# A streaming encoder layer on one core: the opening stages in another order (pool inputs first, in 2 KB rows; forget columns last; input tiles normed and transposed one by one)

## The reference, cut to what matters

```
h = rmsnorm(x, g_mix_pre)                      # x is (384, 2048)
p = h @ w_in                                   # w_in is (2048, 8208)
q, k, v = p[:, 0:1024], p[:, 1024:2048], p[:, 2048:3072]
logf = log_sigmoid(p[:, 3072:3088] + b_f)      # forget columns, one per head
u = p[:, 3088:4112]                            # pool inputs, 4 groups of 256 columns
ga, gb = p[:, 4112:6160], p[:, 6160:8208]
a_out  = softmax(q k^T / 8 + c[t] - c[s]) v    # c = cumulative sum of logf (cache_logf before it)
pooled = windowed means of u (2, 4, 8, 16 rows, with state_pool before it) - u
m = sigmoid(ga) * (a_out @ w_attn_up) + sigmoid(gb) * (pooled @ w_pool) * pool_scale
x = x + rmsnorm(m @ w_out);  y = x + rmsnorm(relu(rmsnorm(x) @ w_ff1)^2 @ w_ff2)
```

## Time and profile before

| | us |
|---|---|
| three runs | 1989.45, 1991.40, 1992.78 |
| median of the runs | 1991.4 |
| profiled execution, its own time | 1990.38 |
| profiled execution, its span | 1988.8 |
| PE busy in the span | 1925.6 |

### The profile page before, as it was taken

How to read it: one execution, slowest core, us unless ns; L and a number is a source line. 1 busy time by engine, 2 the same in 40 slices (tenths; PEclk the granted TensorE clock), 3 DMA queues, 4 the chain that set the end, 5 groups by cost and what they waited for, 6 DMA issues and landing times.

```text
span 1988.8 us, 26585 instructions
## 1 busy us (share of the span) xinstructions
PE 1925.6 (97%) x10576; PEld 1782.7 (90%) x10576; DVE 843.0 (42%) x1064; ACT 661.9 (33%) x896; POOL 188.8 (9%) x242
## 2 busy tenths in 40 slices
PE   3999999999999999997999999999999999999997
PEld 3998999989999998886989989899899898998996
DVE  4644444444333324336444444444444444444446
ACT  4333443433323323335323323223233232232332
POOL 0623323320010102001000000000000000000000
PEclk8999999999999999998999999999999999999999
DMA  6537878855434435342344344343443444434432
GB/s 164 141 94 203 174 193 172 181 149 127 127 127 127 128 127 205 129 128 90 126 129 127 128 127 127 128 127 127 128 127 128 127 127 128 127 127 128 127 127 86
DMA packets 216315, 269.40 MB, mean 135 GB/s; under 512 B 15313, under 2 KB 150705, under 8 KB 215184
## 3 DMA queue, kind: packets, MB, share of 16 engines
q1 hardware_dynamic: 200912, 235.98, 41.6%
q0 software_dynamic: 15296, 31.90, 5.3%
HBM read 260.69 MB, written 7.08 MB: 135 GB/s over the span
## 4 chain that ended last, share of the span: by engine, by line
PE 93%; DMA 3%; DVE 1%; issue 1%; ACT 1%; POOL 1%; SPq 0%; DVEq 0%; ACTq 0%; POOLq 0%
PE ps L459 18%; PE ps L461 18%; PE ps L460 18%; PE ps L479 11%; PE ps L480 11%; PE ps L481 11%; DMA w_raw<-in_w_in_dram 1%; DMA bias_s<-ncs_dram 1%; PE ps L614 1%; DMA out_dram<-u_nat 1%; PE ps L680 0%; PE ps L631 0%; PE ps L835 0%; PE ps L685 0%; DVE w_lo L1261 0%
## 5 line engine op out<-in xcount | busy, mean ns | idle before, releaser
L1261 DVE TENSOR_TENSOR w_lo<-w_raw,w_hi 128x1024 fp32r<-128x1024 f32 x437 | 544.6, 1247 | 864.5 <-ACT w_hi L905 864.3
L905 ACT CAST w_hi<-w_raw 128x1024 fp32r<-128x1024 f32 x437 | 458.5, 1050 | 894.1 <-PE ps L461 453.3
L459 PE MATMUL ps<-ht_hi,w_hi 128*128 128x384 f32 x2064 | 697.6, 338 | 4.8 <-DVE w_lo L1261 3.0
L461 PE MATMUL ps<-ht_hi,w_lo 128*128 128x384 f32 x2064 | 691.1, 335 | 0.0
L460 PE MATMUL ps<-ht_lo,w_hi 128*128 128x384 f32 x2064 | 690.9, 335 | 0.0
L459 PEld LDWEIGHTS ps<-ht_hi,w_hi 128*128 128x128 f32 x2064 | 388.7, 188 | 7.8 <-issue 7.2
L460 PEld LDWEIGHTS ps<-ht_lo,w_hi 128*128 128x128 f32 x2064 | 388.7, 188 | 0.4
L461 PEld LDWEIGHTS ps<-ht_hi,w_lo 128*128 128x128 f32 x2064 | 388.3, 188 | 0.0
L479 PE MATMUL ps<-w_hi,z_hi 128*128 128x512 f32 x762 | 298.8, 392 | 1.8 <-DVE w_lo L1261 1.8
L480 PE MATMUL ps<-w_lo,z_hi 128*128 128x512 f32 x762 | 300.2, 394 | 0.0
L481 PE MATMUL ps<-w_hi,z_lo 128*128 128x512 f32 x762 | 295.7, 388 | 0.0
(11 more groups left out here) (241 smaller groups left out, 1133.2 us busy)
## 6 DMA issues: line engine op xcount, KB each, us to landing
w_raw<-in_w_ff_dram SPq DMA_DIRECT2D x256, 512.0 KB, 3.7
w_raw<-in_w_in_dram SPq DMA_DIRECT2D x130, 512.0 KB, 6.5
w_raw<-in_w_out_dram SPq DMA_DIRECT2D x32, 512.0 KB, 3.7
kc<-in_cache_k_dram POOLq DMA_DIRECT2D x8, 1024.0 KB, 12.3
vc<-in_cache_v_dram POOLq DMA_DIRECT2D x8, 1024.0 KB, 11.7
w_raw<-in_w_attn_up_dram SPq DMA_DIRECT2D x16, 512.0 KB, 3.6
bias_s<-ncs_dram POOLq DMA_DIRECT2D x64, 48.0 KB, 6.8
out_dram<-z_gain SPq DMA_DIRECT2D x6, 512.0 KB, 2.7
```

Of the source, the lines that this page charges most:

```text
L459: pe.matmul(out, wh[:, k, cols], x_hi[:, kk, :], start=(kk == 0), stop=False)
L461: last = pe.matmul(out, wl[:, k, cols], x_hi[:, kk, :], start=False, stop=(kk == k_last))
L905: nc.scalar.copy(w_hi[:, u % RING, :], w_raw[:, u % RAWS, :]).then_inc(hi_ready, 1)
L1261: nc.vector.tensor_tensor(w_lo[:, u % RING, :], w_raw[:, u % RAWS, :], f32(w_hi[:, u % RING, :]), ALU.subtract).then_inc(lo_ready, 1)
```

## The change

The numbers of the units are permuted: `U_U = 0`, `U_F = U_U + 16`, `U_POOL = U_F + 2`. The pool inputs are taken as two halves of eight units with 2 KB rows. The forget chain comes after the pool inputs, spread over the pool stage and the first head pair. What the kernel computes is the same.

```diff
 # SP
-            for t in range(TT):
-                sp.dma_start(x_sb[:, t, :], ...)
             sp.dma_start(gain_nat[:, 0, :], ...)
+            for t in range(2):
+                sp.dma_start(x_sb[:, t, :], xp_v[:, t, :]).then_inc(x_landed[t], 16)
+            sp.dma_start(x_sb[:, 2, 0:D // 2], xs_v[:, 0:D // 2]).then_inc(x_landed[2], 16)
+            sp.dma_start(x_sb[:, 2, D // 2:D], xs_v[:, D // 2:D]).then_inc(x_half_landed, 16)
+            def pool_inputs(g):
+                for q in range(8):
+                    load(U_U + 8 * g + q, 0, win(2 * q, 2, OFF_U + 512 * (1 - g), 512), 2, 512)
+            pool_inputs(0)
             (gain rows 1 and 2)
+            pool_inputs(1)
             for n in range(2):
                 load(U_F + n, 0, win(8 * n, 8, OFF_F, P), 8, P)
-            for s, g in enumerate(ORDER):
-                for n in range(4):
-                    load(U_U + 4 * s + n, 0, win(4 * n, 4, OFF_U + 256 * g, 256), 4, 256)
 # PE
             pe.wait_ge(pool_const, 1)
+            for n in range(10):
+                pe.transpose(ps[:, 0, 0:P], ident[:, :], ident[:, :])
+            (gain row 0 turned) 
+            for n in range(20):
+                pe.transpose(ps[:, 0, 0:P], ident[:, :], ident[:, :])
+            pe.wait_ge(gain_ready, 1)
+            for t in range(TT):
+                pe.wait_ge(xn_ready, t + 1)
+                for k in range(8):
+                    turn_x(t, k)
+                if t < TT - 1:
+                    for n in range(16 - 8 * t):
+                        pe.transpose(ps[:, 7, 3 * P:4 * P], ident[:, :], ident[:, :])
+            for q in range(8):
+                pe.wait_ge(ht_lo_ready, max(4, 2 * q + 2))
+                across(U_U + q, 0, 4, 4, 2 * q, 2, ht_hi, ht_lo, KD - 1)
+                (q < 4: k-tiles 8 + 2q and 9 + 2q turned; q == 6: state, cached logf, gains turned)
+            pe.wait_ge(hist_saved, 2)
+            pe.wait_ge(aux_saved, 2)
+            for q in range(8):
+                across(U_U + 8 + q, 0, 0, 4, 2 * q, 2, ht_hi, ht_lo, KD - 1)
+            for n in range(2):
+                across(U_F + n, 0, 7, 1, 8 * n, 8, ht_hi, ht_lo, KD - 1)
 ...
             pe.wait_ge(brb_act, 2 * GROUPS)
+            head_pair(U_HP, 0, 0, 0, False)
             pe.wait_ge(brb_dve, 2 * GROUPS)
             pe.wait_ge(unat_saved, 4)
-            head_pair(U_HP, 0, 0, 0, False)
+            pe.wait_ge(f_dve, 12)
+            (logf turned, then_inc(fnat_psum, 1)); pe.wait_ge(fnat_saved, 1)
 # ACT
+            act.wait_ge(ones_ready, 1)
+            nc.scalar.activation(root_warm[:, :], ones[:, 0:TT], ACT.Sqrt)
+            (squares: tile 2 only its first half)
             slot(-2, 0)
+            for k in range(4):
+                turned_hi(k)
             slot(-1, 0)
+            (turned_hi 4 to 7; then slot(U_U + q) and two turned_hi for q in 0 to 3)
 ...
+            slot(U_F, 0); slot(U_F + 1, 0)
+            pool_hi(2, ORDER[2])
+            act.wait_ge(f_dve, 3)
+            (f_exp; aux_saved; then U_POOL, with f_log at s == 2)
             head_pair(U_HP, 0, 0, 0, False)
             act.wait_ge(pool_stored, 144)
             act.wait_ge(nc_stored, 144)
+            act.wait_ge(logf_stored, 32)
             head_pair(U_HP + 6, 0, 1, 1, True)
 # DVE
+            (tile 2: tensor_tensor_reduce squares its second half; the tile is scaled in two halves)
+            turned_lo 0, 1; slot(-2); turned_lo 2, 3; slot(-1); turned_lo 4 to 7; then per unit two
 ...
+            slot(U_F, 0); slot(U_F + 1, 0)
+            pool_lo(2, ORDER[2])
+            f steps 1 to 3
+            slot(U_POOL); outs(0); pool_lo(3); slot(U_POOL + 1); f step 4; outs(1); f steps 5 to 7
+            slot(U_POOL + 2); outs(2); un_p and u_nat copies; slot(U_POOL + 3); outs(3)
+            f steps 8 to 12; ncp scan
+            slot(U_HP, 0)
+            slot(U_HP + 1, 0)
+            new_forgets()          # waits logf_new_in 128 and aux_saved; scan, seven copies
+            slot(U_HP + 2, 0)
+            slot(U_HP + 3, 0)
+            keys(0, 0)
+            slot(U_HP + 4, 0)
+            slot(U_HP + 5, 0)
+            (fnat_psum; logf_nat copied out, fnat_saved)
             head_pair(U_HP + 6, 0, 1, 1, True)
 # POOL
-            (b_f, state and cached logf loads first)
+            nc.gpsimd.memset(ones[:, :], 1.0).then_inc(ones_ready, 1)
             (identity, iotas)
+            pool.wait_ge(x_landed[TT - 1], 16)
+            (state, cached logf, b_f loads)
+            (all four windows; nine stores of u)
             pool.wait_ge(unit_used, U_HP)
+            load_keys(0)
+            load_values(0)
             pool.wait_ge(pool_stored, 144)
             (memsets of qp and qs, q_zero)
+            pool.wait_ge(f_dve, 12)
+            for b in range(BD):
+                pool.dma_start(logf_all[...], logf_t[...]).then_inc(logf_new_in, 16)
+            pool.wait_ge(ncp_ready, 1)
+            pool.dma_start(ncp_dram, ncp[:, :]).then_inc(nc_stored, 16)
+            pool.wait_ge(ncs_ready, 2)
+            for b in range(BD):
+                pool.dma_start(ncs_dram[:, b, :, :], ncs[...]).then_inc(nc_stored, 16)
             pool.wait_ge(nc_stored, 144)
             pool.wait_ge(dve_const, 11)
-            load_keys(0)
             load_bias(0)
-            load_values(0)
+            pool.wait_ge(fnat_saved, 1)
+            pool.dma_start(lfp_v, logf_nat[:, 0:2, :]).then_inc(logf_stored, 16)
+            pool.dma_start(lfs_v, logf_nat[:, 2, :]).then_inc(logf_stored, 16)
```

More of the change, by code:

```diff
@@ L741, in _ @@
             pe.wait_ge(brb_act, 2 * GROUPS)
+            head_pair(U_HP, 0, 0, 0, False)
             pe.wait_ge(brb_dve, 2 * GROUPS)
             pe.wait_ge(unat_saved, 4)
[L744 removed]
+            pe.wait_ge(f_dve, 12)
+            for t in range(TT):
+                last = pe.transpose(ps[:, 4, t * H:(t + 1) * H], logf_t[:, t * P:(t + 1) * P], ident[0:H, 0:H])
+            last.then_inc(fnat_psum, 1)
+            pe.wait_ge(fnat_saved, 1)
             head_pair(U_HP + 6, 0, 1, 1, True)
@@ new lines, in _, with f_step @@
+            for q in range(8):
+                slot(U_U + 8 + q, 0)
+                if q == 3:
+                    pool_lo(0, ORDER[0])
+                elif q == 6:
+                    pool_lo(1, ORDER[1])
+            slot(U_F, 0)
+            slot(U_F + 1, 0)
+            pool_lo(2, ORDER[2])
+            dve.wait_ge(unit_used, U_F + 2)
+            dve.wait_ge(bf_landed, 16)
+            steps = [0]
+            def f_step(ins):
+                steps[0] += 1
+                ins.then_inc(f_dve, 1)
+                dve.wait_ge(f_dve, steps[0])
@@ new lines, in _ @@
+            for n in range(2):
+                dve.wait_ge(unat_psum, n + 3)
+                nc.vector.tensor_copy(u_nat[:, 512 * n:512 * n + 512], ps[:, 6 + n, :]).then_inc(unat_saved, 1)
+            slot(U_POOL + 3, 0)
+            outs(3, ORDER[3])
+            f_step(nc.vector.tensor_tensor(f_abs[:, :], f_abs[:, :], f_exp[:, :], ALU.mult))
+            dve.wait_ge(f_act, 2)
+            f_step(nc.vector.tensor_tensor(f_abs[:, :], f_abs[:, :], f_log[:, :], ALU.mult))
+            f_step(nc.vector.scalar_tensor_tensor(out=f_log[:, :], in0=f_x[:, :], scalar=0.0, in1=f_exp[:, :],
+                                                  op0=ALU.is_equal, op1=ALU.mult))
@@ L1563, in head_pair, with new_forgets @@
                     out_sample(a)
-            head_pair(U_HP, 0, 0, 0, False)
+            def new_forgets():
+                dve.wait_ge(logf_new_in, 128)
+                dve.wait_ge(aux_saved, 1)
+                nc.vector.tensor_tensor_scan(ncs[:, 0:PAST + QS], ones[:, :], logf_all[:, :], 0.0,
+                                             ALU.mult, ALU.subtract).then_inc(ncs_ready, 1)
+                dve.wait_ge(ncs_ready, 1)
+                for b in range(1, BD):
+                    last = nc.vector.tensor_copy(ncs[:, PAST + QS * b:PAST + QS * (b + 1)],
+                                                 ncs[:, PAST:PAST + QS])
+                last.then_inc(ncs_ready, 1)
+            slot(U_HP, 0)
[6 more added lines that the diff above has]
+            slot(U_HP + 5, 0)
+            dve.wait_ge(fnat_psum, 1)
+            nc.vector.tensor_copy(logf_nat[:, :, :].rearrange("p t h -> p (t h)"),
+                                  ps[:, 4, 0:TT * H]).then_inc(fnat_saved, 1)
             head_pair(U_HP + 6, 0, 1, 1, True)
```

349 lines of the change are left out of this document (167 added, 182 removed).

## The result

| | before | after |
|---|---|---|
| median of the runs (5 each) | 1992.78 us (1989.45 to 1993.86) | 2001.69 us (1999.67 to 2004.01) |
| ratio to before | | 1.0047, 95% interval 1.0036 to 1.0059 |
| span of the profiled execution | 1988.8 us | 2000.3 us |
| PE busy | 1925.6 us | 1938.6 us |
| second pair of sample scores | 187.81 us | 197.65 us |

The change made the kernel 0.47% slower. The last two rows say where: the loss lies in the first 200 us (the second pair comes 9.8 us later, the median is 8.9 us longer), and the rest takes as long as before to about 1 us.

What follows compares the result with a forecast made beforehand. PE, busy 1925.6 of 1988.8 us, was taken as the bound, leaving only its gaps and clock. The opening's gain was lost in POOL's queue, net +7.6: 1990.4 + 7.6 = 1998.0, 1999.0 on the median's scale; range 1985 to 2011.

Steps and rivals of the forecast that it cites:

- main case: Opening's gain lost in POOL's queue before the sample scores: +3 to +14 us, 1994 to 2006, chance 0.48.
- Part 1: Opening: PE's unit stream starts at 21.8 us, 14.7 earlier, with 1.7 us of half clock charged.
- Parts 2 and 3: Pool inputs end at 94.1 us; pool stage, with two forget units and 2.8 us of new waits, at 123.6.
- Part 4, step 2: POOL's queue after the pool stage: stores of u land in 12.2 us, at 141.6; logf copies issued by 147.0.
- Step 3: Log-forget copies on POOL's queue, behind key and value loads, land at about 153 us, bounds 149.7 and 160.
- Step 4: DVE's scan and copies (1.08 + 2.04), then a low part (1.23): PE resumes at 157.4 us, having stood 17.
- Step 5: POOL's scan stores issue in 4.5 us and land in 2.2 (162.9); bias lands in 6.6, at 174.9.
- Step 7: PE waits for ACT's values copy after units five to eight; sample scores at 189.3 us, +7.6 against 181.70.
- Rival A: POOL's chain lands quickly, stores of u within 8 us, most of the opening kept: -4 to -10, about 1984; chance 0.26.
- B: Opening's gain and POOL-queue loss cancel within 4 us, one landing of four shorter being enough: 1991; chance 0.12.
- C: Long queue of keys, values and 512 B head loads; copies land at 160, bias 15 us: +23, about 2014; chance 0.12.
- D: Pool inputs: 2 KB rows also bring only 55 GB/s, a unit each 9.5 us against 4.16: about 2080; chance 0.02.

Runs made afterwards that it cites:

- x11: Changed kernel with SyncE's w_in loads from the head pairs' ninth unit on held until the scan's stores have landed: 2002.05 us, 1.0054.
- x1: Changed kernel with DVE's scan of the new log forgets moved from before the fifth head unit's low part to behind the eighth: 2001.40 us, 1.0052.
- x3: Changed kernel with POOL's log-forget copies and prompt-sum store issued before the key and value loads and the wait for the stores of u: 1994.60 us, 1.0013.
- x4: Changed kernel with the key loads issued just before the bias and the value loads just behind it: 2009.0 us, 1.0089.
- x7: Changed kernel with the 16 pool-input loads in 512 B rows instead of 2 KB rows, same bytes in all: 2006.42 us, 1.0077.
- x9: Changed kernel without its 54 transposes of the identity in the opening: 2001.42 us, 1.0055.

## Why the prediction was right

It said 1999.0 us and 1994 to 2006 for the main case; measured 2001.69. By its own steps:

- **Part 1.** Stream at 21.8: measured 21.84. Half clock there for some 3 us (1.7 charged): 0.50 from 22 to 24.6 us, up to 27 in other traces of the same opening, and keeping the clock up ended the pool inputs 1.0 to 3.1 us sooner. The identity transposes (54, where the prediction speaks of 30) as a thing that lifts the clock: as the trace shows below, yes, but it had fallen again before it counted.
- **Parts 2 and 3.** Pool inputs over at 94.1 (94.20), pool stage at 123.6: the stores of u were issued by 129.49 against the 129.4 worked out.
- **Part 4, step 2**, stores of u landing in 12.2: 10.5. **Step 3**, copies landing in 6.0: 7.2, within its bounds. **Step 4**: PE resumed at 154.3 instead of 157.4; besides the shorter landing, the scan and its copies took 1.4 us where I had used the 3.1 of the earlier trace rows. There POOL was adding window sums at the same time, here it wasn't working; that this is the reason wasn't tried.
- **Step 5** was mis-sized most. Landing of the scan's stores: 2.2 taken, 12.06 measured. Landing of the bias: 6.6 taken, 3.3 measured. The first was read from the earlier trace rows, where SyncE's queue took 25.4% of the engines at that time; at 157 to 169 us it took 52.1%. The upper end of the main case (+13) had it at 4. That SyncE's loads make this landing is shown by x11. Why they are so many at this moment can be read from the trace, but no run tried it alone: a slot comes free with DVE's low part, and DVE stood 19.0 us for `logf_all`. SyncE's longest wait is the same stretch:

```profile
SPq L364 <- DVE w_lo L1313: 63.0, 12, 19.5
```

  At 154.2 us, when DVE's low parts go on, SyncE issues two loads within 1.5 us and a third at 157.1, while POOL issues the scan's stores (153.3 to 157.7). In x1, where DVE didn't stand there and SyncE waited for 3.8 us at most from 120 to 180 us, the stores landed in 8.0. The share of the engines alone doesn't order the cases: in x3 SyncE's queue took 62.1% and the stores landed in 7.2.
- **Step 6.** ACT released at 180.1: 181.82. **Step 7.** Sample scores at 189.3: 191.81, so +10.1 instead of +7.6, and the measured median is 2.7 us above the forecast. That it came so near is in part luck: step 5 had the stores 9.9 us too short, and against that stood the 3.1 us by which the scan was over sooner and the 3.3 us by which the bias landed sooner.
- **Rival A**, the chain lands quickly, needed the stores of u within 8 us; they took 10.5. **B**, level, wanted one landing of four shorter; one was (the bias), but another was 10 us longer. **C** wanted the copies landed at 160 us and 15 us for the bias; they landed at 151.6, and it took 3.3. A long queue there was, but at the scan's stores, and by x4 not made by the keys. **D**, row length: x7 excludes the 9.5 us a unit on which it rested.

**The rate of 512 B rows** was misread too. The trace has 54 to 56 GB/s for them, and I took this for a rate that such rows are bound to. It isn't: in x7 they kept PE busy for 70.1 of 72 us, with 118 GB/s on all queues together. The Trainium skill, DMA: Bandwidth & Descriptors, Specifications, says that 512 B is the least transfer for line rate; by it 512 B rows would cost no more engine time for a byte than longer ones. x7's 1.7 times speaks against that, but its total of +4.7 us says that little hung on it.

## What to carry to other kernels

Before moving a stage back, list the small transfers that then come one behind another on a path with nothing else in it: each costs its landing, and a landing read where the DMA engines are idle doesn't hold where a bulk queue is on. A wait of the engine that frees the load buffers (DVE here) also stops the bulk loads, and when it ends several go out at once: look at which small transfer is issued then. That such a transfer is always the one that waits longest isn't shown; in the kernel before, the bias took 15.7 us. And look for the one blocking instruction in the old order first: moving one slot got as much as the new order did at its best.

## What the hardware did that I had not expected

- **Transposes alone raise the granted clock.** PE by microsecond in the changed kernel, in a stretch in which it runs nothing but transposes:

```profile
12.00:13.00 1.00, 1.00 (x6) 0.50 1.05 401
13.00:14.00 1.00, 1.00 (x7) 0.50 1.07 279
14.00:15.00 1.00, 1.00 (x8) 0.72 1.08 199
15.00:16.00 1.00, 1.00 (x12) 1.00 1.01 184
```

  0.50 is 1.2 GHz and 1.00 is 2.4. The Trainium skill, TensorE: Matmul & The Clock Gate, part 4, says that full clock doesn't engage for transposes; here the record and the pace (6 to 12 transposes a microsecond) both say that it does. In x9, without those of the identity, PE turned 7 in the microsecond from 18, with the record at 1.00.
- **The record can say 1.00 at half pace.** x9's rows above have 1.00 throughout at 3 to 5 matmuls a microsecond; its first matmul of the stream took 0.69 us, as long as the one that the changed kernel ran at 0.50. Early in an execution the pace is the better witness.
- **The same 24 KB stores landed in 1.8, 4.3, 7 to 9 and 12 us**, with no change in the stores. The 1.8 and 4.3 are the two runs that hold SyncE's loads back; what sets 7 against 12 among the others wasn't tried.
- **512 B rows at 55 GB/s with most DMA engines idle.** From 97 to 103 us SyncE's loads moved 55 GB/s with 29.7% of the engines taken in the changed kernel, while rows of the same length kept PE busy in x7. What sets the 55 wasn't tried.
